# Opening expert group with its chunks in another order, the second gather behind four chunks, counts behind the ranks, and router logits straight from x

## What is computed

```
x = x + (g_a * branch_a + g_b * branch_b) @ w_out
hm = rmsnorm(x, norm_ffn)
logits = hm @ w_router + b_router
top_v, top_i = top_k(logits, 4)
gates = one_hot(top_i) * softmax(top_v)        # 264 x 32
for e in range(32):
    gu = hm @ w_gate_up[e] + b_gate_up[e]      # 1024 -> 2048
    gate, up = min(gu[:, :1024], 7), clip(gu[:, 1024:], -7, 7)
    hid = (up + 1) * (gate * sigmoid(1.702 * gate))
    out += gates[:, e] * (hid @ w_down[e] + b_down[e])
x = x + out
```

## Time and profile before

| | before |
|---|---|
| three timed runs, median (lowest to highest) | 1419.71 us (1417.78 to 1431.76) |
| span of the profiled execution | 1417.1 us |
| busy in it: PE / PEld / DVE / ACT / POOL | 1342.0 / 749.9 / 477.7 / 291.1 / 26.6 us |
| read from HBM | 455.78 MB |
| transfers, mean over the span | 327 GB/s |
| mean granted TensorE clock | 0.993 |

### The profile page before, as it was taken

How to read it: one execution, slowest core, us unless ns; L and a number is a source line. 1 busy time by engine, 2 the same in 40 slices (tenths; PEclk the granted TensorE clock), 3 DMA queues, 4 the chain that set the end, 5 groups by cost and what they waited for, 6 DMA issues and landing times.

```text
span 1417.1 us, 21577 instructions
## 1 busy us (share of the span) xinstructions
PE 1342.0 (95%) x8363; PEld 749.9 (53%) x8363; DVE 477.7 (34%) x1203; ACT 291.1 (21%) x673; POOL 26.6 (2%) x64
## 2 busy tenths in 40 slices
PE   8999999999999999999999898898989899999996
PEld 7877777768885444434434434344333434534355
DVE  3666868763235221122122211212212022121224
ACT  4645453525012100000001000001000000101024
POOL 3000000000000000000000000000000000000000
PEclk9999989999999999999999999999999999999998
DMA  7325243453767999999999999999999999999971
GB/s 220 139 91 154 92 123 151 153 209 122 294 230 277 405 421 420 421 420 421 421 420 419 421 421 421 421 421 422 421 420 421 420 421 416 420 421 421 420 292 32
DMA packets 86524, 463.23 MB, mean 327 GB/s; under 512 B 11141, under 2 KB 29086, under 8 KB 33326
## 3 DMA queue, kind: packets, MB, share of 16 engines
q1 hardware_dynamic: 70229, 452.99, 78.9%
q10 hardware_dynamic: 16193, 8.84, 2.2%
HBM read 455.78 MB, written 6.68 MB: 326 GB/s over the span
## 4 chain that ended last, share of the span: by engine, by line
PE 62%; DMA 21%; SPq 6%; DVE 5%; ACT 3%; issue 2%; ACTq 0%; POOL 0%; DVEq 0%; POOLq 0%
PE bank L1213 18%; DMA ring<-in_w_gate_up 16%; PE bank L1258 11%; PE bank L1021 10%; SPq L630 6%; PE bank L1153 5%; DMA ring<-in_w_down 4%; PE bank L1068 3%; PE bank L1283 2%; PE bank L1102 2%; PE bank L1326 2%; DMA dedicated<-in_w_gate_up 2%; DVE lent L2025 1%; PE bank L1267 1%; PE bank L849 1%
## 5 line engine op out<-in xcount | busy, mean ns | idle before, releaser
L1213 PE MATMUL bank<-ring,lent 128*64 128x512 f32 (+1 forms) x1832 | 385.7, 598 | 34.7 <-DMA ring<-in_w_gate_up 34.2
L1213 PEld LDWEIGHTS bank<-ring,lent 128*64 128x64 f32 (+1 forms) x1832 | 120.1, 131 | 249.5 <-issue 247.8
L1021 PE MATMUL bank<-lent,ring 128*128 128x264 f32 x896 | 231.3, 400 | 5.1 <-ACT lent L1613 1.6
L1258 PE MATMUL bank<-ring,lent 128*64 128x512 f32 (+1 forms) x928 | 182.7, 594 | 3.0 <-DMA ring<-in_w_down 3.0
L1021 PEld LDWEIGHTS bank<-lent,ring 128*128 128x128 f32 x896 | 163.1, 192 | 41.1 <-issue 10.2
L1698 ACT ACTIVATE big<-big 128x256 f32<-128x256 f32 x64 | 26.7, 417 | 509.2 <-DVE big L2196 509.2
L2196 DVE TENSOR_SCALAR big<-bank 128x256 f32<-128x256 f32 x64 | 27.0, 423 | 268.8 <-PE bank L1213 268.8
L1258 PEld LDWEIGHTS bank<-ring,lent 128*64 128x64 f32 (+1 forms) x928 | 58.0, 129 | 112.3 <-issue 111.0
L1153 PE MATMUL bank<-st,big 88*128 88x128 f32 x768 | 88.9, 275 | 0.6 <-ACT pair_space L1704 0.5
L1153 PEld LDWEIGHTS bank<-st,big 88*128 88x128 f32 x768 | 87.2, 192 | 3.0 <-issue 1.6
L2215 DVE TENSOR_TENSOR xT<-xT,bank 128x264 f32<-128x264 f32 x128 | 54.9, 429 | 96.6 <-PE bank L1283 78.1
(11 more groups left out here) (438 smaller groups left out, 1397.8 us busy)
## 6 DMA issues: line engine op xcount, KB each, us to landing
ring<-in_w_gate_up SPq DMA_DIRECT2D x205, 1024.0 KB, 23.5
ring<-in_w_down SPq DMA_DIRECT2D x100, 1024.0 KB, 24.1
ring<-in_w_in SPq DMA_DIRECT2D x28, 1024.0 KB, 5.0
dedicated<-in_w_gate_up SPq DMA_DIRECT2D x13, 1024.0 KB, 23.8
dedicated<-in_w_down SPq DMA_DIRECT2D x9, 1024.0 KB, 24.1
late<-in_w_gate_up SPq DMA_DIRECT2D x8, 1024.0 KB, 22.9
outputs<-in_w_gate_up SPq DMA_DIRECT2D x7, 1024.0 KB, 24.9
lent<-in_w_gate_up SPq DMA_DIRECT2D x7, 1024.0 KB, 22.3
```

What stands on the lines that cost most here:

```text
L1021: last = mm(b[:, 0:T], w[:, k, o:o + P], aT[:, k, :], start=k == 0, stop=k == KD - 1)
L1213: last = mm(bank[q][lo:hi, :], x_slots[:, 4 * half + k, lo:hi], w, start=False, stop=half == 1 and k == 3)
L1258: last = mm(bank[4 + t][lo:hi, :], hT[:, m, lo:hi], w, start=m == 0, stop=m == KD - 1)
```

## The change

Four edits.

1. **Chunk order of the opening group.** `OPENING = [0, 2, 4, 6, 1, 3, 5, 7]` is the order of c on PE, and of the loads g = 0 to 15. Half 1 is gathered, and the gates are transposed, ahead of the fifth c instead of the second. Bank q then completes with the fifth to eighth c, and DVE's first piece waits for 12 used chunks.
2. **Homes.** `ONCE_AT = [10, 11]`: the two places that are used once hold chunks 10 and 11 (before 2 and 3). The loads keep their places in the SP queue, and carry other chunks: slots 5 and 6 now hold 2 and 3, slots 0 and 1 hold 12 and 13. So loads 23 to 30 wait for chunks 2 to 9 instead of 4 to 11. The load of chunk 14 waits for the last token transposes (`hm5`) instead of the logits.
3. **Router.** The raw logits are made from `xT`, and DVE multiplies the router weights by the norm's scale once, in the conformer part (step `silu`). The last raw logits no longer wait for ACT. The part of the sums of squares without the last block is done ahead, and the transposes of the last two token blocks are moved behind the sums and behind the logits. ACT scales the token pieces in the order 0, 2, 4, 1, 3, 5, and the first gather waits for pieces 0, 2, 4 alone.
4. **Counts.** They get a use of bank 0 (`count`) of their own, so that the ranks are released ahead of them.

```diff
-BEFORE = {20: [17], 21: [18], 25: [13, 4], 26: [7, 8], 32: [0, 1], 33: [12, 5], 34: [6, 19]}
+BEFORE = {20: [17], 21: [18], 25: [3, 4], 26: [7, 8], 32: [0, 1], 33: [2, 5], 34: [6, 19]}
+OPENING = [0, 2, 4, 6, 1, 3, 5, 7]
+ONCE_AT = [10, 11]
...
         plan("rank", 1)
+        plan("count", 0)
...
-        for i, name in zip((2, 3), ONCE):
+        for i, name in zip(ONCE_AT, ONCE):
...
-                load_chunk(experts[i % 2], i // 2, places(home_of[g]), loaded_of(home_of[g]))
+                c = OPENING[i // 2] if g < 2 * KD else i // 2
+                load_chunk(experts[i % 2], c, places(home_of[g]), loaded_of(home_of[g]))
...
-            load_first(2)
+            load_first(10)
             wait_used(sp, len(stream) - 2)
-            load_first(10)
+            load_first(12)
             wait_used(sp, len(stream) - 1)
+            load_first(13)
             load_first(11)
-            load_first(3)
             load_first(20)
-            to_drain(sp, "logits")
+            to_drain(sp, "hm5")
...
-                return mm(b[q, 0:T], wr[:, k, :], xg[:, k, :], start=k < 4, stop=k >= 4)
+                return mm(b[q, 0:T], wr[:, k, :], xT[:, k, :], start=k < 4, stop=k >= 4)
...
-                if i:
+                if 0 < i < KD - 1:
                     tokens_of(i - 1)
-            pe.wait_ge(s["wr_loaded"], 16 * 2)
             lqb = to_fill(pe, "lq")
             for k in range(KD - 1):
                 raw_logits(lqb, k)
-            pe.wait_ge(s["xg_ready"], KD)
+            pe.wait_ge(s["sums_ready"], 1)
+            b = to_fill(pe, "ss")
+            for j in range(NTB):
+                mm(b[0:TB, 2 * j:2 * j + 2], sq_sum[:, j * TB:(j + 1) * TB], ones[:, 0:2], start=j == 0, stop=False)
+            wait_drained(pe, f"wo{KD - 1}")
             fill_done("lq", raw_logits(lqb, KD - 1))
...
-            tokens_of(KD - 1)
+            tokens_of(KD - 2)
             wait_drained(pe, "lq")
...
             fill_done("logits", last)
+            tokens_of(KD - 1)
...
-            mm(b[0:TB, 2 * NE:3 * NE], ones[0:TB, 0:TB], sel[:, 1, :], start=False, stop=True)
+            fill_done("rank", mm(b[0:TB, 2 * NE:3 * NE], ones[0:TB, 0:TB], sel[:, 1, :], start=False, stop=True))
+            b = to_fill(pe, "count")
             for i in range(NTB):
-                last = mm(b[:, NTB * NE:(NTB + 1) * NE], ones[0:TB, :], sel[:, i, :], start=i == 0, stop=i == NTB - 1)
-            fill_done("rank", last)
-            for i in range(2, 8):
+                last = mm(b[:, 0:NE], ones[0:TB, :], sel[:, i, :], start=i == 0, stop=i == NTB - 1)
+            fill_done("count", last)
+            for i in (2, 4, 6):
                 pe.wait_ge(drained[i], before_experts[i])
...
-                for c in range(KD):
-                    if opening and c == 0:
+                for at, c in enumerate(OPENING if opening else range(KD)):
+                    if opening and at == 0:
                         pe.wait_ge(sm["x_ready"], 1)
-                    elif opening and c == 1:
+                    elif opening and at == 4:
                         gather(sm, 0, (1,))
                         gates_to_rows()
                         pe.wait_ge(sm["x_ready"], 2)
...
                     elif n == "silu":
+                        dve.wait_ge(s["wr_loaded"], 16 * 2)
+                        tell(v.tensor_tensor(wr[:], wr[:], par[:, 8:16].unsqueeze(2).broadcast_to([P, KD, NE]), ALU.mult))
                         dve.wait_ge(s["csig"], 1)
...
-                    dve.wait_ge(sm["chunk_used"], at * RING + 4 * (q + 1))
+                    dve.wait_ge(sm["chunk_used"], max(KD + 2 * (q + 1), ONCE_AT[-1] + 1) if sm is first_pass and first
+                                else at * RING + 4 * (q + 1))
```

More of the change, by code:

```diff
@@ L1109, in _ @@
                 raw_logits(lqb, k)
[L1110 removed]
+            pe.wait_ge(s["sums_ready"], 1)
[3 more added lines that the diff above has]
+            wait_drained(pe, f"wo{KD - 1}")
             fill_done("lq", raw_logits(lqb, KD - 1))
             pe.wait_ge(s["squares"], 2)
[L1113 removed]
             for j in range(NTB):
[L1115 to L1117 removed]
+                last = mm(b[0:TB, 2 * j:2 * j + 2], sq_last[:, j * TB:(j + 1) * TB], ones[:, 0:2], start=False, stop=j == NTB - 1)
             fill_done("ss", last)
[L1119 removed]
+            tokens_of(KD - 2)
             wait_drained(pe, "lq")
@@ L1211, in group @@
                         for i, (x, lo, hi) in enumerate(tiles):
-                            w = weights(sems, n, 2 * c + x, k * 512)
+                            w = weights(sems, n, 2 * at + x, k * 512)
                             last = mm(bank[q][lo:hi, :], x_slots[:, 4 * half + k, lo:hi], w, start=False,
@@ L1305, in _ @@
             pe.wait_ge(s["bias_ready"], 1)
-            for i in range(2):
+            for i in (0, 1, 3, 5, 7):
                 pe.wait_ge(drained[i], before_experts[i])
@@ L1665, in _ @@
             act.wait_ge(s["rstd_ready"], 2)
-            for i in range(6):
+            for i in (0, 2, 4, 1, 3, 5):
                 b = to_drain(act, f"hm{i}")
@@ L2106, in _ @@
                     tell(v.tensor_tensor(sq[i % 2], x, x, ALU.mult))
-                    tell(v.tensor_tensor(sq_sum, sq_sum, sq[i % 2], ALU.add))
+                    tell(v.tensor_tensor(sq_sum, sq_sum, sq[i % 2], ALU.add), "sums_ready" if i == KD - 2 else None)
                 else:
@@ L2135, in _ @@
             b = to_drain(dve, "rank")
-            tell(v.scalar_tensor_tensor(rank, b[0:TB, 0:NTB * NE].rearrange("p (j e) -> p j e", j=NTB), FAR, sel[:],
-                                        ALU.add, ALU.mult))
+            out_of(v.scalar_tensor_tensor(rank, b[0:TB, 0:NTB * NE].rearrange("p (j e) -> p j e", j=NTB), FAR, sel[:],
+                                          ALU.add, ALU.mult), "rank")
             dve.wait_ge(s["consts"], CONSTS + 2)
             PER = 8
+            first_pass = first
             def quarter(x, q):
```

13 lines of the change are left out of this document (4 added, 9 removed).

## The result

| | before | after |
|---|---|---|
| median of 11 timed runs each (lowest to highest) | 1420.06 us (1417.78 to 1431.76) | 1428.44 us (1425.00 to 1429.78) |
| ratio, with its 95% interval | | 1.0052 (1.0038 to 1.0066) |
| span of the profiled execution | 1417.1 us | 1423.6 us |

What follows compares the result with a forecast made beforehand. Weight transfers were taken to bound the kernel, with the end following chunk 16's use. From the profiled 1417.1 us: + 10.4 - 1.1 - 6.9 + 1.7 = 1421.2, plus 2.6 to the median: 1423.8 us; range 1416.0 to 1428.5.

Steps and rivals of the forecast that it cites:

- What bounds: Whole kernel: the weight transfers bind, so the end follows the use of chunk 16, which releases load 35.
- the 14 loads: Opening group: 14 loads can be out before load 35, as before; they need 35.0 us of transfer.
- The gap at 448: Transfers in the opening group: this gap closes, 5.7 us taken alone, but is given back at 480.
- The gather position: Opening group: DVE places experts later, PE waits 3.5 us, and the gather of group 1 starts 2.4 us later.
- Rival D: Opening group: placing the experts does not hold PE, so only the router part reaches the end; 1418.6 us, chance 0.06.
- C: Transfers in the opening group: the gain from closing the gap at 448 us is kept; 1412.9 us, chance 0.06.
- B: Gather of group 1: experts are placed late but the clock does not fall; 1422.1 us, chance 0.20.
- Router and counts: Router, ahead of the first gather: start earlier by 1.1 us, bounds 0.3 and 1.9.
- The clock: Gather of group 1: PE's clock falls behind its 3.5 us wait, costing 1.7 us, priced from one later row.
- A: Opening group, the forecast case: experts placed late and a fall of the clock; 1423.8 us, chance 0.60.
- rival E: Gather through down chunks: the clock stays low, costing 18.7 us with the late placing; 1438.4 us, chance 0.03.
- the high end: Whole kernel, top of the range: 1428.5 us, from a smaller router gain, a doubled clock price and run spread.

Runs made afterwards that it cites:

- gates_early: Changed kernel with the gates' transposes and their copy put back behind the first c of the opening group; 1420.85 us, ratio 1.0006 against before.
- gates_down: gates_early with two blocks of hidden rows and two down steps moved ahead of the gather of group 1; 1413.32 us, ratio 0.9953 against before.
- router_only: Changed kernel with chunk order, homes, loads and second gather put back, keeping the router and counts edits; 1419.29 us, ratio 0.9995 against before.
- before_down: Kernel before with two blocks of hidden rows and two down steps moved ahead of the gather of group 1; 1416.20 us, ratio 0.9977.
- before_gates_late: Kernel before with only the gates' transposes moved, from ahead of c = 1 to ahead of c = 4; 1430.30 us, ratio 1.0076.
- after_filled_behind: Changed kernel with eight unread matmuls behind PE's wait for the one-hot of group 1, ahead of its gather; 1428.37 us in one run.
- after_down: Changed kernel, gates still late, with two blocks of hidden rows and two down steps ahead of the gather of group 1; 1422.91 us, ratio 1.0026.
- after_filled: Changed kernel with eight unread matmuls filling PE's wait ahead of the gather of group 1; 1422.46 us, ratio 1.0018 against before.
- after_half_filled: Changed kernel with four unread matmuls filling part of PE's wait ahead of the gather of group 1; 1422.16 us in one run.
- gates_hidden: gates_early with only the first two blocks of hidden rows moved ahead of the gather of group 1; 1416.00 us, ratio 0.9974 against before.

## Why the prediction was right, and where it was short

**What bounds, and the 14 loads: right.** The span less the issue of load 35 is 933.0 to 934.0 us in eight kernels, before and after among them, over issue times from 483.96 to 494.84. The gap at 448 closed and opened again behind it: the issues of loads 21 to 28 come in four pairs one c apart (439.39 to 449.69) and those of 29 to 32 in two more (456.90 and 463.76), the transfers run at 410 to 438 GB/s from 442 to 472 us and at 397 and 346 in the four us behind, and end near 476, which is 479 us with the head start of 2.9 us added, as predicted. Then they stand until the issue at 490.61. That issue was forecast for 486 to 488 and comes at 493.5 with the head start added, so the gap is some 14.5 us long and not 6 to 8. It is later than the sum has it (483.96 + 2.4 + 1.7 = 488.1) by what the clock (4.6) and the router (0.9) fell short by, as below. By the Trainium skill, page "Perfetto Trace Analysis", section "Optimization Strategy", the gap on the bound resource was the thing to remove by starting its release sooner. gates_early did just that and had 1.0006 (0.9996 to 1.0015); the rule became true only in gates_down, when the next release no longer came last.

**The gather position: right.** Predicted 18.7 us of idle time on DVE and a wait of 3.5 us on PE; measured 19.63 and 3.39. The start of the gather of group 1 moved by 3.25 us, where the sum had 2.4; the difference is the router's. Rival D (the placing off the path) is out, and so are C (the closed gap kept) and B (the clock kept).

**Router and counts: 1.1 us predicted, 0.2 us measured.** The hop over ACT did go, but the last raw logits could not use it. The timeline of after, PE in the router:

```profile
422.74 1.09 PE L1099 MATMUL bank<-xT,smalls 128*32 128x264 f32 x14
423.76 0.63 PE L1116 MATMUL bank<-ones,outputs 128*88 128x2 f32 x6
424.32 0.63 PE L1099 MATMUL bank<-xT,smalls 128*32 128x264 f32 x2
...
426.48 3.28 PE L1094 MATMUL bank<-pT,ones 128*128 128x264 f32 x14
```

By its timeline DVE had the last block of x ready at 423.35; PE came to it at 424.32, behind the seven other raw logits and the three early sums that the change put ahead of it (each matmul has two records). The logits (L1127) start at 425.71, or 33.63 us behind the output projection's start, against 33.74 before. I took 0.8 us off there by counting what the data no longer waits for, and did not lay out what PE itself had to issue between. The transposes behind the logits then hold the unread matmuls as predicted, and these end 0.16 us later than before instead of 0.4 sooner. Only the counts gave what was left.

**The clock: 1.7 us predicted, 6.3 us measured.** This is the step that failed, and in size alone: A was the right case. Even the bound of twice the row's price, 3.4 us, was too low. The term came from one c after a wait of 2.45 us, behind which the clock was back within 4 us. Here it stayed low over the gather (9.77 us from its start to that of the hidden rows, against 5.47 before: 4.3 us), over the hidden rows (5.24 against 4.60: 0.6) and over the first down c up to the issue of load 35 (5.04 against 3.68: 1.4). These add up to 6.3. I had written the mechanism down as rival E, the clock staying down, and priced the gather in it at 5.4 us, but gave it 0.03, since the only row lasted under 4 us. The truth lies between: low for 17 us, up again within the first down c, so that the loads behind load 35 were not delayed on top.

That the median still lies inside the range is luck. The terms of the high end add up to 1423.8 + 0.8 + 1.7 + 2 = 1428.3 us, written as 1428.5; with the terms as measured (0.9 more for the router, 4.6 for the clock) the sum would have been 1429.3 us, outside the range. The measured time came out 0.9 us below that, as the times moved by less than load 35 did; the cause of this is argued below and not shown.

By the Trainium skill, page "TensorE: Matmul & The Clock Gate", section "HAM oscillation — how this bites in real kernels", the penalty is the time at the lower level times one half. By that rule 17 us would cost 8.5 us, an estimate. The trace has 6.3, and the measurement decides. Nearly all of the difference lies in the 5.24 us of the hidden rows, where PE waited for DVE twice (1.34 and 1.07 us): there the low clock cost 0.6 us and not half of the time.

**Sum, corrected:** 10.4 - 0.2 - 6.9 + 6.3 = 9.6 us at load 35, where the table has 9.55. The times moved by 7.4 us (5.4 to 9.4). The 2 us between may lie in the profiled execution of before, whose clock was at 1.00 behind the hidden rows: router_only and gates_early, with the same work there and no wait ahead of the gather, show a fall of some 3 us and have load 35 at 90.41 and 90.93 instead of 88.98. If most executions of before have that fall, their load 35 stands near 90.5, and the shift to after is 8. The trace of before is of one execution, so this is argued and not shown. What is shown is that executions differ in this way at another place (last section).

## What to carry to other kernels

Before moving an instruction, list what stands behind its consumer in the queues of the in-order engines: here three small transposes moved by three c held 17 us of unrelated DVE work. Where a fixed number of transfers can be outstanding, closing a gap ahead of the release that comes last only moves the gap; bring that release forward first (before_down), and then close the gap (gates_down). And a fall of TensorE's clock is to be priced by the work that stands behind the wait in its own place, with the case that it stays low through all of it, and not by one row from another part of the kernel.

## What was not expected of the hardware

After a wait of 3.4 to 3.7 us TensorE's clock stayed at 1.2 GHz for 17 us in after and some 20 us in before_gates_late. PE's records show it busy without a pause for the first eight of them in after (472 to 480 us) and for ten in before_gates_late (474 to 484 us), and then with two short waits among the work. In after_filled_behind the same wait was followed by the unread matmuls, and the clock was back in 3 us. In after_down it rose some 5 us into the down c that began at 478.27 (0.64 in the 2 us from 482), in after some 3 us into those that began at 485.57. Which property of the work decides is not settled by these runs.

Much shorter waits were followed by a fall too. Behind two waits of 1.5 and 1.3 us among the hidden rows the clock was at the lower level for 3.4 us in gates_early, router_only, after_filled and after_half_filled, for some 7 us in after_filled_behind, and not at all in the profiled execution of before, which has the same waits (1.53 and 1.27 us). In gates_hidden, gates_down and before_down, where these waits are gone, it stayed at 1.00.

The same wait need not have the same effect in two executions. At 315 us (318 in before) all twelve kernels have PE wait 2.22 or 2.23 us for DVE and then run the same eight records: 2.05 us in before and after, whose clock was 1.00 there, and 3.04 to 3.74 us in the ten others, where it was 0.83 in the ten us from 310. From that row to the output projection it is 77.1 us in before and after and 78.6 to 78.8 in the others. Between before and before_gates_late nothing differs in the program up to there, so an execution can lose some 1.5 us in this way at one place.
